# A gated feed-forward's up-projection with both halves of the activation as one 512-column moving operand

## The chip, the cores and the metric

The kernel runs on one core of a Trainium2 chip. The metric is the device time of one execution in microseconds; three executions of the kernel before took 1926.08, 1931.16 and 1932.69 us (median 1931.16). A profile is one further execution, recorded instruction by instruction.

## What is computed

One sequence of 256 tokens, 1024 wide, goes through two blocks of two layers each, all in float32. Six feed-forwards are in it: four gated ones (two in each layer of the first block), which the change touches, and two with a convolution (second block), which it does not touch.

```python
def swiglu(h, w_gate, w_up, w_down):
    return (jax.nn.silu(h @ w_gate) * (h @ w_up)) @ w_down
...
    for i in range(DEPTH):                       # DEPTH = 2
        ...
        h = modulate(rms_norm(x, norm_g[i, 0]), shift[:, 0], scale[:, 0])
        x = x + MACARON_WEIGHT * gate[:, 0, None, :] * swiglu(h, ffn_w_gate[i, 0], ffn_w_up[i, 0], ffn_w_down[i, 0])
        ... # attention
        h = modulate(rms_norm(x, norm_g[i, 2]), shift[:, 2], scale[:, 2])
        x = x + MACARON_WEIGHT * gate[:, 2, None, :] * swiglu(h, ffn_w_gate[i, 1], ffn_w_up[i, 1], ffn_w_down[i, 1])
```

`h` is 256 x 1024, `w_gate` and `w_up` are 1024 x 2816, `w_down` is 2816 x 1024.

## The kernel before

**Numbers in two parts.** TensorE takes its operands as fp32r. Each float32 operand is split into a high part (what fp32r keeps) and a low part (the rest), and a product is made of three matmuls: low activation by high weight, high activation by high weight, high activation by low weight. In the code `h_hi` and `h_lo` are the parts of the activation, `w_hi` and `ring_lo` those of the weight.

**The weight stream.** All weights of the program come in one stream, cut into quarters of 128 x 1024 floats. SyncE loads halves (two quarters) into a ring of four slots. For each quarter ScalarE copies the high part into `w_hi` (L1051, four buffers), and then VectorE subtracts it, in place, to leave the low part in `ring_lo` (L1461). TensorE signals `quarter_done` behind each quarter; ScalarE may split quarter q once quarter q - 4 is done, and SyncE may reload a slot once both of its quarters are done.

**A gated feed-forward** (`ffn` on each engine, called with f = 0 to 3) has 11 steps of up-projection and then 22 quarters of down-projection. A step makes 256 hidden columns of the gate and 256 of the up matrix, from four quarters of weights. `up_turned` holds a 128 x 128 block of weights stationary and streams 256 columns (the tokens) through it: four quarters, two chunks `i` in each, four blocks `b`, three matmuls, so 96 matmuls of 256 columns in a step (L496 to L498). The four blocks accumulate in two banks of PSUM, two blocks side by side: the gate in bank `b`, the up half in bank `b + 1`, with `b` 0 or 2 in turn (`UP_BANKS`). The conv feed-forwards use `up_turned` as well.

**At the end of a step** ScalarE takes the silu of the gate bank into `wa` (L1130), VectorE multiplies it by the up bank into `wb` (L1632, signals `h_ready`), ScalarE copies the high part of the product before this one (`keep_hi`, L1120), and VectorE subtracts to get its low part (`keep`, L1617). Each engine runs its instructions in the order in which they are written: per step ScalarE has four splits, then silu and `keep_hi`; VectorE has four splits with two pieces of other work between them in f = 0 to 2 (`mod_turn`, L1497: columns of the modulation vectors for later layers), then the multiplication and `keep`. Splits run three quarters ahead of TensorE (`LEAD`). TensorE begins step j once `h_ready` of step j - 2 is there.

The **down-projection** (`quarter`, L463 to L465, and `down_last`, L517 to L519) streams 512 columns of weights past a stationary 128 x 128 block of the hidden activation: 12 matmuls of 512 columns in a quarter.

Of the kernel before, what the change touches and what calls it, by code (L numbers as in the profile page):

```python
# [97 lines left out]
POOL_Q = [BASE[_f] + 4 * _j + 5 for _f in ("ffn4", "ffn5") for _j in range(UPS)]  # L98
UP_BANKS = (0, 2)
MIX_BANKS = (0, 2, 4, 0)  # L100
DOWN_BANK = 2
# [71 lines left out]
def build(nc, a, out):  # L173
    ctx = ExitStack()
    with ctx:
# [25 lines left out]
        hT = over("hT", slab_at["hT"], [P, KC, T])  # L201
        h_lo = over("h_lo", slab_at["hT"], [P, KC, T], F32R)
        h_hi = over("h_hi", slab_at["h_hi"], [P, KC, T], F32R)
        arena = over("arena", slab_at["arena"], [P, ARENA])
# [110 lines left out]
        x_ready, x_half = sem("x_ready"), sem("x_half")  # L315
        ms_ready, xn_ready, norm_T, norm_hi, norm_lo = sem("ms_ready"), sem("xn_ready"), sem("norm_T"), sem("norm_hi"), sem("norm_lo")
        silu_ready, h_ready, hid_ready_all = sem("silu_ready"), sem("h_ready"), sem("hid_ready_all")
        fgate_ready, fconv_ready, gelu_ready = sem("fgate_ready"), sem("fconv_ready"), sem("gelu_ready")
# [124 lines left out]
        def _(pe):  # L443
# [39 lines left out]
            def up_turned(q, bank, it, per, fresh):  # L483

                for r in range(4):
# [13 lines left out]
                    mm.then_inc(quarter_done, 1)  # L499

            def down(q, kk, count, parts, bank):

                def lhs(i, tt):
                    return parts(kk, tt)
                quarter(q + kk, None, 0, lhs, lambda i, tt: ps[:, bank + 2 * tt + i, :], lambda i: kk == 0, lambda i: kk == count - 1, kk == count - 1)
# [59 lines left out]
            def ffn(f, conv, m):  # L565
# [3 lines left out]
                def step(j, it):  # L569
                    if v0 + j >= RING or it is not None:  # L570

                        pe.wait_ge(fconv_ready if conv else h_ready, val(it, v0 + j - RING + 1))
                    up_turned(q0 + 4 * j, UP_BANKS[j % 2], it, TURNQ, (norm_lo, 8 * m) if j == 0 else None)

# [8 lines left out]
                for kk in range(DOWNQ):  # L583
                    if kk % 2 == 0:
                        pe.wait_ge(hid_ready_all, UPS * f + kk // 2 + 1)
                    if f < 3 and kk in GATES[f]:
                        gates(*GATES[f][kk])
                    if kk < DOWNQ - TAIL:
                        down(q0 + UPQ, kk, DOWNQ, hid_parts, DOWN_BANK)
# [450 lines left out]
        def _(act):  # L1040
# [81 lines left out]
            def ffn(f):  # L1122
                q0 = BASE[f"ffn{f}"]

                def step(j, it):
                    u, b = UPS * f + j, UP_BANKS[j % 2]
                    split_step(q0 + 4 * j, it, TURNQ)
                    act.wait_ge(quarter_done, val(it, q0 + 4 * j + 4, TURNQ))
                    act.wait_ge(h_ready, val(it, u))
                    nc.scalar.activation(wa[:, 0:512], ps[:, b, :], ACT.Silu).then_inc(silu_ready, 1)  # L1130
                    if j > 0:
                        keep_hi(f, j - 1, it)
                for j in range(PEEL):
# [313 lines left out]
        def _(dve):  # L1447
# [159 lines left out]
            def ffn(f):  # L1607
# [11 lines left out]
                def step(j, it):  # L1619
                    u, b = UPS * f + j, UP_BANKS[j % 2]  # L1620
                    for r in range(4):
                        split(q0 + 4 * j + LEAD + r, q0 + 4 * j + LEAD + r + 1, it, 4 * turn)
                        if mod and r % 2 == 1:
# [4 lines left out]
                            else:  # L1628
                                mod_turn(t, it, MOD_UP * (j - peel) + r // 2)
                    dve.wait_ge(silu_ready, val(it, u + 1, turn))  # L1630
                    half = (j % 2) * 512
                    v.tensor_tensor(wb[:, half:half + 512], ps[:, b + 1, :], wa[:, 0:512], ALU.mult).then_inc(h_ready, 1)  # L1632
                    if j > 0:
                        keep(j - 1, it)

                for j in range(peel):
                    step(j, None)
                with dve.Fori(0, UPS // turn) as it:
                    tick.enter(it, 1 if mod else 0)
                    for r in range(turn):  # L1640
# [698 lines left out]
```

## Time and profile before

| | us |
|---|---|
| median of 3 executions | 1931.16 |
| the profiled execution, its time | 1931.93 |
| its span, first to last instruction | 1930.3 |
| TensorE busy | 1819.3 (94%) |
| VectorE busy | 1420.4 (74%) |
| ScalarE busy | 940.5 (49%) |
| up-projections of the gated feed-forwards | 39 to 168, 398 to 525, 593 to 722, 1115 to 1244 |

The span leaves out 1.6 us around the first and last instruction. The granted TensorE clock has a mean of 0.977 over the span. A matmul's own duration in the trace overlaps with that of its neighbours, so the time that a stream of matmuls takes is read from the distance between their starts.

### The profile page before, as it was taken

To read this page: it belongs to the slowest core of one execution; us is meant where nothing else is said; L and a number is where in the kernel's file an instruction comes from. 1 tells how busy PE (TensorE), PEld (TensorE's weight loads), DVE (VectorE), ACT (ScalarE), POOL (GpSimd) and SP (SyncE) were. 2 spreads that over 40 slices of the span, in tenths; PEclk is the share of its full clock that TensorE was granted. 3 is DMA by queue.
4 is the path that set the end of the run, shared out by engine and by line. 5 is a ranking of instruction groups with operands and counts; after the bars stand their busy time and mean duration, and the time that the engine had idled before them with its cause. 6 is when DMAs were issued, how large, how long until landed. Compare 5 with 4: busy or idle time off the path is not lost.

```text
span 1930.3 us, 31852 instructions
## 1 busy us (share of the span) xinstructions
PE 1819.3 (94%) x11710; PEld 1620.2 (84%) x11710; DVE 1420.4 (74%) x2280; ACT 940.5 (49%) x1360; POOL 128.5 (7%) x168
## 2 busy tenths in 40 slices
PE   2999999889999999999999999999889999979998
PEld 2999777789988997788878799987679987769996
DVE  6778798687778778877665565548869866877894
ACT  3444465454435443555454454445764445664443
POOL 0001010000010000000000000000011100001110
PEclk8999999899999999999999999999999999999999
DMA  9878765457787778454540165545144554324553
GB/s 383 289 277 294 269 230 197 140 186 271 276 306 271 276 267 282 170 175 175 191 155 1 48 233 184 185 175 207 66 177 176 187 185 164 117 88 164 185 180 125
DMA packets 63267, 382.62 MB, mean 198 GB/s; under 512 B 7088, under 2 KB 7088, under 8 KB 26688
## 3 DMA queue, kind: packets, MB, share of 16 engines
q1 hardware_dynamic: 42624, 300.96, 43.3%
q0 software_dynamic: 19984, 77.93, 11.2%
q10 hardware_dynamic: 576, 2.60, 0.3%
q8 instruction: 55, 0.90, 0.2%
q14 instruction: 28, 0.23, 0.0%
HBM read 380.42 MB, written 1.05 MB: 198 GB/s over the span
## 4 chain that ended last, share of the span: by engine, by line
PE 86%; DVE 8%; ACT 4%; issue 2%; DMA 1%; SPq 0%; DVEq 0%; ACTq 0%
PE ps L496 13%; PE ps L497 13%; PE ps L498 13%; PE ps L463 11%; PE ps L465 11%; PE ps L464 11%; DVE ring_lo L1461 1%; PE ps L764 1%; PE ps L517 1%; PE ps L519 1%; PE ps L518 1%; PE ps L790 1%; PE ps L777 1%; PE ps L544 1%; DMA arena<-in_mod 1%
## 5 line engine op out<-in xcount | busy, mean ns | idle before, releaser
L1461 DVE TENSOR_TENSOR ring_lo<-ring,w_hi 128x1024 fp32r<-128x1024 f32 x534 | 647.7, 1222 | 341.4 <-ACT w_hi L1051 336.7
L1051 ACT ACTIVATE w_hi<-ring 128x1024 fp32r<-128x1024 f32 x556 | 584.2, 1057 | 601.2 <-PE ps L498 307.6
L496 PE MATMUL ps<-h_lo,w_hi 128*128 128x256 f32 x2112 | 602.3, 285 | 13.0 <-DVE ring_lo L1461 11.4
L497 PE MATMUL ps<-h_hi,w_hi 128*128 128x256 f32 x2112 | 601.3, 285 | 0.0
L498 PE MATMUL ps<-h_hi,ring_lo 128*128 128x256 f32 x2112 | 600.9, 285 | 0.0
L496 PEld LDWEIGHTS ps<-h_lo,w_hi 128*128 128x128 f32 x2112 | 409.4, 194 | 14.5 <-DVE ring_lo L1461 11.6
L497 PEld LDWEIGHTS ps<-h_hi,w_hi 128*128 128x128 f32 x2112 | 409.5, 194 | 0.0
L498 PEld LDWEIGHTS ps<-h_hi,ring_lo 128*128 128x128 f32 x2112 | 409.2, 194 | 0.0
L463 PE MATMUL ps<-w_hi,h_lo 128*128 128x512 f32 x604 | 246.2, 408 | 13.8 <-DVE h_lo L1873 6.4
L464 PE MATMUL ps<-ring_lo,h_hi 128*128 128x512 f32 x604 | 238.9, 396 | 0.0
L465 PE MATMUL ps<-w_hi,h_hi 128*128 128x512 f32 x604 | 238.7, 395 | 0.0
L463 PE MATMUL ps<-w_hi,hid_lo 128*128 128x512 f32 x456 | 180.0, 395 | 0.0
L465 PE MATMUL ps<-w_hi,hid_hi 128*128 128x512 f32 x456 | 177.5, 389 | 0.0
L464 PE MATMUL ps<-ring_lo,hid_hi 128*128 128x512 f32 x456 | 177.5, 389 | 0.0
L463 PEld LDWEIGHTS ps<-w_hi,h_lo 128*128 128x128 f32 x604 | 115.8, 192 | 42.2 <-issue 8.2
L465 PEld LDWEIGHTS ps<-w_hi,h_hi 128*128 128x128 f32 x604 | 115.6, 191 | 25.4
L464 PEld LDWEIGHTS ps<-ring_lo,h_hi 128*128 128x128 f32 x604 | 115.8, 192 | 22.3
L1497 DVE CUSTOM_DVE_ANT_0 arena<-arena 128x1024 f32<-128x1024 f32 x94 | 114.1, 1219 | 13.8 <-ACT cact L1410 11.1
L405 POOL DMA_DIRECT2D arena<-in_mod x128 | 67.7, 529 | 658.3 <-DVE arena L1497 376.0
L463 PEld LDWEIGHTS ps<-w_hi,hid_lo 128*128 128x128 f32 x456 | 85.6, 188 | 18.9 <-issue 1.2
L464 PEld LDWEIGHTS ps<-ring_lo,hid_hi 128*128 128x128 f32 x456 | 85.6, 188 | 18.8 <-issue 1.4
L465 PEld LDWEIGHTS ps<-w_hi,hid_hi 128*128 128x128 f32 x456 | 85.6, 188 | 17.9
(322 smaller groups left out, 1888.9 us busy)
## 6 DMA issues: line engine op xcount, KB each, us to landing
ring<-in_stream SPq DMA_DIRECT2D x278, 1024.0 KB, 4.8
arena<-in_mod POOLq DMA_DIRECT2D x128, 512.0 KB, 5.6
arena<-in_mod SPq DMA_DIRECT2D x14, 512.0 KB, 15.6
gate<-in_wide POOLq DMA_DIRECT2D x3, 1536.0 KB, 10.0
arena<-in_nsaw POOLq DMA_DIRECT2D x2, 1072.0 KB, 9.2
arena<-in_konst POOLq DMA_DIRECT2D x1, 1295.5 KB, 9.5
arena<-in_mixw POOLq DMA_DIRECT2D x2, 576.0 KB, 10.6
x<-in_x ACTq DMA_DIRECT2D x1, 1024.0 KB, 12.7
```

The source lines that it names most:

```text
L405: pool.dma_start(mring[:, r, :], a["mod"][q, :, r * QUARTER:(r + 1) * QUARTER]).then_inc(mod_in[r], 16)
L463: nc.tensor.matmul(dst, x_lo, hi, start=first(i), stop=False)
L464: nc.tensor.matmul(dst, x_hi, lo, start=False, stop=False)
L465: mm = nc.tensor.matmul(dst, x_hi, hi, start=False, stop=last(i))
L496: nc.tensor.matmul(dst, hi, x_lo, start=(r == 0 and i == 0 and b % 2 == 0), stop=False)
L497: nc.tensor.matmul(dst, hi, x_hi, start=False, stop=False)
L498: mm = nc.tensor.matmul(dst, lo, x_hi, start=False, stop=(r == 3 and i == 1 and b % 2 == 1))
L517: nc.tensor.matmul(dst, x_lo, hi, start=False, stop=False)
L518: nc.tensor.matmul(dst, x_hi, lo, start=False, stop=False)
L1051: nc.scalar.activation(w_hi[:, q % SPLITS, :], ring[:, half % SLOTS, (q % 2) * QUARTER:(q % 2 + 1) * QUARTER], ACT.Copy).then_inc(w_hi_rea ...
L1461: v.tensor_tensor(ring_lo[:, slot, cs], ring[:, slot, cs], w_hi[:, q % SPLITS, :], ALU.subtract).then_inc(w_lo_ready, 1)
L1497: return v.tensor_tensor_reduce(out=junk[n % 2], in0=src, in1=crow, scale=1.0, scalar=0.0, op0=ALU.mult, op1=ALU.add, accum_out=to)
```

## The change

The two parts of the activation become two halves of one tile, `h_both`; in memory they lie where they lay. In steps 1 to 10 of the four gated feed-forwards a new function, `up_wide`, takes the place of `up_turned`. One matmul streams 512 columns, the low and then the high part, through the high weight into one whole PSUM bank; a second one of 256 columns adds high activation by low weight to the upper half of that bank. Each of the four blocks has a bank of its own, and two sets of four banks take turns (`WIDE_BANKS`). What was one sum is now in two halves of a bank. ScalarE copies the lower halves of two banks at a time to `wa`, VectorE adds the upper halves to them, and the silu and the multiplication then read `wa` and not PSUM. Step 0 stays as it was, since it takes the activation as it is made. `gates` in the down-projection uses banks 6 and 7 and so waits for the last step's product.

```diff
+WIDE_BANKS = ((0, 1, 6, 7), (2, 3, 4, 5))
...
-        h_lo = over("h_lo", slab_at["hT"], [P, KC, T], F32R)
-        h_hi = over("h_hi", slab_at["h_hi"], [P, KC, T], F32R)
+        h_both = over("h_both", slab_at["hT"], [P, 2, KC, T], F32R)
+        h_lo, h_hi = h_both[:, 0, :, :], h_both[:, 1, :, :]
...
+            def up_wide(q, banks, it, per):
+
+                for r in range(4):
+                    low_part(q + r, it, per)
+                    slot, half, buf = ((q + r) // 2) % SLOTS, ((q + r) % 2) * QUARTER, (q + r) % SPLITS
+                    for i in range(2):
+                        for b in range(4):
+                            o = i * 512 + b * P
+                            hi, lo = w_hi[:, buf, o:o + P], ring_lo[:, slot, half + o:half + o + P]
+                            nc.tensor.matmul(ps[:, banks[b], :].rearrange("p (w t) -> p w t", w=2), hi, h_both[:, :, 2 * r + i, :],
+                                             start=(r == 0 and i == 0), stop=False)
+                            mm = nc.tensor.matmul(ps[:, banks[b], T:2 * T], lo, h_hi[:, 2 * r + i, :], start=False, stop=(r == 3 and i == 1))
+                    mm.then_inc(quarter_done, 1)
...
+                    if f < 4 and j > 0:
+                        up_wide(q0 + 4 * j, WIDE_BANKS[j % 2], it, TURNQ)
+                        return
                     up_turned(q0 + 4 * j, UP_BANKS[j % 2], it, TURNQ, (norm_lo, 8 * m) if j == 0 else None)
...
                     if f < 3 and kk in GATES[f]:
+                        pe.wait_ge(h_ready, UPS * (f + 1))
                         gates(*GATES[f][kk])
... (ScalarE)
                     act.wait_ge(h_ready, val(it, u))
-                    nc.scalar.activation(wa[:, 0:512], ps[:, b, :], ACT.Silu).then_inc(silu_ready, 1)
-                    if j > 0:
-                        keep_hi(f, j - 1, it)
+                    if j == 0:
+                        nc.scalar.activation(wa[:, 0:512], ps[:, b, :], ACT.Silu).then_inc(silu_ready, 1)
+                        return
+                    for n, b in enumerate(WIDE_BANKS[j % 2][::2]):
+                        low = ps[:, b:b + 2, 0:T]
+                        nc.scalar.activation(wa[:, n * 512:(n + 1) * 512].rearrange("p (b t) -> p b t", b=2), low, ACT.Copy).then_inc(low_kept, 1)
+                    keep_hi(f, j - 1, it)
+                    act.wait_ge(gate_whole, val(it, (UPS - 1) * f + j))
+                    nc.scalar.activation(wa[:, 0:512], wa[:, 0:512], ACT.Silu).then_inc(silu_ready, 1)
... (VectorE)
+                    half = (j % 2) * 512
+                    if j == 0:
+                        dve.wait_ge(silu_ready, u + 1)
+                        v.tensor_tensor(wb[:, half:half + 512], ps[:, b + 1, :], wa[:, 0:512], ALU.mult).then_inc(h_ready, 1)
+                        return
+                    for n, b in enumerate(WIDE_BANKS[j % 2][::2]):
+                        dve.wait_ge(low_kept, val(it, 2 * ((UPS - 1) * f + j - 1) + n + 1, 2 * turn))
+                        low = wa[:, n * 512:(n + 1) * 512].rearrange("p (b t) -> p b t", b=2)
+                        ins = v.tensor_tensor(low, ps[:, b:b + 2, T:2 * T], low, ALU.add)
+                        if n == 0:
+                            ins.then_inc(gate_whole, 1)
+                        else:
+                            tick.mark(ins)
+                    keep(j - 1, it)
                     dve.wait_ge(silu_ready, val(it, u + 1, turn))
-                    half = (j % 2) * 512
-                    v.tensor_tensor(wb[:, half:half + 512], ps[:, b + 1, :], wa[:, 0:512], ALU.mult).then_inc(h_ready, 1)
-                    if j > 0:
-                        keep(j - 1, it)
+                    tick.settle()
+                    v.tensor_tensor(wb[:, half:half + 512], wa[:, 512:1024], wa[:, 0:512], ALU.mult).then_inc(h_ready, 1)
```

How the order of the instructions changes is shown at two places. The first is on TensorE, where step 0 of the first gated feed-forward ends and step 1 begins. Before:

```order
L496 MATMUL ps<-h_lo,w_hi 128x256
L497 MATMUL ps<-h_hi,w_hi 128x256
L498 MATMUL ps<-h_hi,ring_lo 128x256
L496 MATMUL ps<-h_lo,w_hi 128x256 [waits w_lo_ready]
L497 MATMUL ps<-h_hi,w_hi 128x256
```

After (the names of both parts of the activation now read `h_both`):

```order
L498 MATMUL ps<-h_both,w_hi 128x256
L499 MATMUL ps<-h_both,w_hi 128x256
L500 MATMUL ps<-h_both,ring_lo 128x256
L512 MATMUL ps<-h_both,w_hi 128x512 [waits w_lo_ready]
L514 MATMUL ps<-h_both,ring_lo 128x256
```

From step 1 on the three matmuls of a block are two, the first of them twice as wide; the wait for the weight's low part stands where it stood.

The second place is on VectorE, at the end of a step in the loop of the same feed-forward, behind the last piece of modulation work. Before:

```order
L1497 ISA arena<-arena 128x1024 [waits mod_used]
L1497 ISA arena 128x1
L1630 ISA
L1632 TENSOR_TENSOR wb<-ps,wa 128x512 [waits silu_ready]
L1615 REGISTER_ALU
L1617 ISA [waits hid_hi_ready]
L1617 TENSOR_TENSOR hid_lo<-wb,hid_hi 128x512
L1459 REGISTER_ALU
L1461 TENSOR_TENSOR ring_lo<-ring,w_hi 128x1024 [waits w_hi_ready]
```

After:

```order
L1523 ISA arena<-arena 128x1024 [waits mod_used]
L1523 ISA arena 128x1
L1664 TENSOR_TENSOR wa<-ps,wa 128x512 [waits low_kept] x2
L1641 ISA
L1643 ISA [waits hid_hi_ready]
L1643 TENSOR_TENSOR hid_lo<-wb,hid_hi 128x512
L1670 REGISTER_ALU
L164 REGISTER_ALU [waits silu_ready]
L1672 TENSOR_TENSOR wb<-wa 128x512 [waits dve_tick]
L1485 REGISTER_ALU
L1487 TENSOR_TENSOR ring_lo<-ring,w_hi 128x1024 [waits w_hi_ready]
```

Two additions, each with a wait for a copy by ScalarE, stand ahead of everything else at a step's end; the multiplication has moved behind `keep`, and the next quarter's split behind both.

## Rows read from the trace of the kernel before

**Rows 1.** The page: busy time and share of each engine, and the chain's shares.
```profile
span 1930.3 us, 31852 instructions
PE 1819.3 (94%) x11710; PEld 1620.2 (84%) x11710; DVE 1420.4 (74%) x2280; ACT 940.5 (49%) x1360; POOL 128.5 (7%) x168
PE 86%; DVE 8%; ACT 4%; issue 2%; DMA 1%; SPq 0%; DVEq 0%; ACTq 0%
```

**Rows 2.** Busy time by stretch, with count, clock, DMA share, GB/s (steps 1 to 10).
```profile
core 0: us, PE busy (x) PEld busy (x) DVE busy (x) ACT busy (x) POOL busy (x), PEclk, DMA share, GB/s
53.00:168.00 115.00, 115.00 (x961) 115.00 (x960) 84.91 (x104) 51.88 (x59) 10.56 (x20) 1.00 0.77 277
410.00:525.50 115.50, 115.50 (x965) 115.50 (x964) 87.06 (x106) 52.04 (x60) 11.08 (x21) 1.00 0.76 276
1126.00:1244.00 118.00, 118.00 (x984) 117.96 (x983) 62.89 (x60) 54.12 (x62) 0.00 (x0) 1.00 0.51 182
```

**Rows 3.** Waits in 53 to 168 us: total us, times, longest.
```profile
POOL arena L405 <- DVE arena L1497: 99.0, 19, 5.2
ACT w_hi L1051 <- PE ps L498: 44.4, 30, 1.8
DVE ring_lo L1461 <- ACT w_hi L1051: 27.9, 30, 1.7
ACT wa L1130 <- PE ps L498: 17.6, 10, 1.9
```

**Rows 4.** Timeline of ScalarE (start us, duration us): four silus, a step apart.
```profile
87.69 0.60 ACT L1130 ACTIVATE wa<-ps 128x512 f32<-128x512 f32 x1 [1.91 <-PE ps L498]
...
122.24 0.60 ACT L1130 ACTIVATE wa<-ps 128x512 f32<-128x512 f32 x1 [1.90 <-PE ps L498]
```

**Rows 5.** Timeline of TensorE: up-projection's end, down-projection's start and last matmul of L465.
```profile
1243.36 0.28 PE L497 MATMUL ps<-h_hi,w_hi 128*128 128x256 f32 x1
1243.48 0.28 PE L498 MATMUL ps<-h_hi,ring_lo 128*128 128x256 f32 x1
1243.60 0.40 PE L463 MATMUL ps<-w_hi,hid_lo 128*128 128x512 f32 x1
...
1295.08 0.39 PE L465 MATMUL ps<-w_hi,hid_hi 128*128 128x512 f32 x1
```

**Rows 6.** Timeline of TensorE: from 512 columns to 256, and to a smaller stationary block.
```profile
1401.96 0.40 PE L465 MATMUL ps<-w_hi,h_hi 128*128 128x512 f32 x1
1402.19 1.02 PE L1010 MATMUL ps<-arena 128*128 128x256 f32 x4
...
309.68 0.39 PE L465 MATMUL ps<-w_hi,h_hi 128*128 128x512 f32 x1
310.00 0.81 PE L670 MATMUL ps<-arena 64*128 64x256 f32 x6
```

**Rows 7.** Groups by line: count, busy us, mean ns of one.
```profile
L1461 DVE TENSOR_TENSOR ring_lo<-ring,w_hi 128x1024 fp32r<-128x1024 f32 x534 | 647.7, 1222 | 341.4 <-ACT w_hi L1051 336.7
L1632 DVE TENSOR_TENSOR wb<-ps,wa 128x512 f32<-128x512 f32 x44 | 30.4, 691 | 16.0 <-ACT wa L1130 13.9
L1130 ACT ACTIVATE wa<-ps 128x512 f32<-128x512 f32 x44 | 26.4, 600 | 78.0 <-PE ps L498 78.0
L1120 ACT ACTIVATE hid_hi<-wb 128x512 f32 x40 | 24.9, 622 | 0.0
L1690 DVE SCALAR_TENSOR_TENSOR wb<-ps,cols,wb 128x255 f32<-128x255 f32 x88 | 38.0, 473 | 0.0
```

**Rows 8.** Timeline of VectorE around the end of a step of the first gated feed-forward.
```profile
98.47 1.22 DVE L1497 CUSTOM_DVE_ANT_0 arena<-arena 128x1024 f32<-128x1024 f32 x1
99.62 0.08 DVE L1497 DVE_READ_ACCUMULATOR2_ANT arena<- 128x1 f32 x1
99.85 0.17 DVE L1549 COPY arena<-arena 128x4 f32 x1 [0.16 <-DVE arena L1497]
99.96 0.69 DVE L1632 TENSOR_TENSOR wb<-ps,wa 128x512 f32<-128x512 f32 x1
100.57 0.68 DVE L1617 TENSOR_TENSOR hid_lo<-wb,hid_hi 128x512 f32 x1
101.29 1.23 DVE L1461 TENSOR_TENSOR ring_lo<-ring,w_hi 128x1024 fp32r<-128x1024 f32 x1
```

**Rows 9.** Timeline of ScalarE at the same step's end.
```profile
99.20 0.60 ACT L1130 ACTIVATE wa<-ps 128x512 f32<-128x512 f32 x1 [1.90 <-PE ps L498]
99.69 0.62 ACT L1120 ACTIVATE hid_hi<-wb 128x512 f32 x1
100.21 1.05 ACT L1051 ACTIVATE w_hi<-ring 128x1024 fp32r<-128x1024 f32 x1
```

More of the change, by code:

```diff
@@ L316, in build @@
         ms_ready, xn_ready, norm_T, norm_hi, norm_lo = sem("ms_ready"), sem("xn_ready"), sem("norm_T"), sem("norm_hi"), sem("norm_lo")
+        low_kept, gate_whole = sem("low_kept"), sem("gate_whole")
         silu_ready, h_ready, hid_ready_all = sem("silu_ready"), sem("h_ready"), sem("hid_ready_all")
@@ L1638, in ffn @@
                 with dve.Fori(0, UPS // turn) as it:
-                    tick.enter(it, 1 if mod else 0)
+                    tick.enter(it, (1 if mod else 0) + turn)
                     for r in range(turn):
```

## The prediction

> **What bounds the kernel now.** I read the page's head first: TensorE is busy for 94% of the span and carries 86% of the chain that ended last [rows 1]. Such a share is a mean, so the stretches that the change touches come next. In steps 1 to 10 of the gated feed-forwards TensorE is busy without a break (115.00 of 115.00 us), at the full clock, in the feed-forwards with modulation work as in the one without, while VectorE is busy 84.91 us, ScalarE 51.88 and the DMA engines 0.77 of the time [rows 2]. The list of waits of that stretch holds no wait of TensorE at all: the others wait, VectorE for ScalarE's splits, and ScalarE for TensorE to free its buffers [rows 3]. So only what shortens TensorE's own work counts here, until another engine's work for a step is longer than TensorE's.
>
> **What a matmul costs.** Three steps lie between the first and last silu shown, 122.24 - 87.69 = 34.55 us, or 11.52 a step; with 96 matmuls in a step one takes 120.0 ns [rows 4]. The 512-column matmuls of a down-projection: from 1243.60 to 1295.08 lie 227 distances (19 quarters of 12), 51.48 us, so 226.8 ns each [rows 5]. At 2.4 GHz, the level that a granted clock of 1.00 stands for, 256 columns need 106.7 ns and 512 need 213.3. Both kinds leave the same rest, 13.3 and 13.4 ns. I read it as a fixed part of each matmul that does not grow with the columns.
>
> **Part 1, three matmuls become two.** A block's group took 3 x 120.0 = 360.0 ns; it now takes 226.8 + 120.0 = 346.8, and 13.2 ns go. There are 4 feed-forwards x 10 steps x 8 chunks x 4 blocks = 1280 groups, so 1280 x 13.2 ns = 16.9 us. The streamed columns are the same (768 a group); only one fixed part is saved. A step becomes 32 x 346.8 = 11.10 us, 0.42 less.
>
> The trace of before has no stream in which both widths alternate, so the pair is bounded by rows. That a switch of width can be free is seen both ways: 256 columns followed by 512 start 0.12 us apart, 512 followed by 256 on a full block 0.23 [rows 5, 6]. The dearest switch in the rows is 0.32 us, from a 512-column matmul to one on a 64-row block [rows 6]; that would add 0.09 to each group. At the cheap end the 256-column matmul loses its rest too (106.7 ns, a group of 333.5), and 1280 x 26.5 = 33.9 us go. I take the free switch, since the new pair keeps one block shape and one type.
>
> The Trainium skill, "TensorE: Matmul & The Clock Gate", section "Back-to-back issue gap", gives N / 2.4 + 2.5 ns for a warm matmul, so 109.2 ns for 256 columns and 215.8 for 512. The rows show 120.0 and 226.8, so the trace does not agree: the rest is 13.3 here, not 2.5. By the page a group would save 2.5 ns and the change an estimated 3.2 us.
>
> **Part 2, the copies on ScalarE.** Two copies of 512 elements from PSUM are added to each step, 2 x 0.60 by the silu that reads as much from there [rows 7]. ScalarE has 5.2 us of work in a step (51.88 / 10, rows 2); with 1.2 more it is 6.4 of 11.10. Nothing on the path by volume.
>
> **Part 3, the additions on VectorE.** Two of 512 elements with one operand in PSUM, 0.69 each by the multiplication of that shape [rows 7]. VectorE's 8.5 us a step (84.91 / 10) become 9.9 of 11.10, 89%. The dearer bound is 0.95 each, from 473 ns for 255 elements out of PSUM [rows 7]; that makes 10.4. The multiplication reads SBUF now and keeps 0.69. So volume hides it in either case, with 0.7 to 1.2 us to spare in a step of the three feed-forwards with modulation work. The fourth has 62.89 us of VectorE work in 118.00, and far more room [rows 2].
>
> **Part 4, the longer way at a step's end.** This is an added wait, so I follow who stands behind it. Before, with TensorE's step ending at about 99.15, silu runs 99.20 to 99.80, the product 99.96, `keep` 100.57, and the split of the quarter after is done at 102.52, 3.4 us behind the step's end [rows 8, 9]. After: ScalarE's two copies end at 0.65 and 1.15 us; VectorE is free from its modulation work at about 0.9 (99.85 + 0.17, a tenth later since the step is shorter), adds until 1.6 and 2.2, `keep` ends at 2.9; ScalarE's silu, which must wait for the first addition, runs 1.7 to 2.3; the product ends at 3.6, and the split, which queues behind it, at 4.8. That is 1.4 us later. What waits for it: this split is of the last quarter of the step that TensorE has just begun, three quarters of 2.77 us further on, so it is needed at 8.3. It has 3.5 us to spare. ScalarE's split of that quarter moves from about 2.1 to 3.4 us behind the step's end and is done before VectorE asks. From 4.8 VectorE works 1.2 (split), 1.3 (modulation) and 1.2 (split), and it is at 8.5 when ScalarE's fourth split (allowed at 8.3, done at 9.5) makes it wait again. So it has caught up within the step, and nothing adds up from step to step.
>
> TensorE itself waits for the product of two steps before; that comes 3.6 us behind its step's end, against 11.10. The wait added ahead of `gates` wants the last product, 3.6 us into the down-projection; the earliest place is three quarters in, 3 x 12 x 0.227 = 8.2 us. Both at nothing. If this cover were gone, each microsecond of it would be paid once in a step. DMA: the same bytes in 96.4% of the time, 277 to 287 GB/s at a share near 0.80 [rows 2]. Nothing.
>
> **The sum.** 1931.93 (the profiled execution) - 16.9 = 1915.0 us. The median of before is 0.8 below that execution, so I expect 1914.3 as a median.
>
> **The rivals.**
>
> A. *The fixed part does not go.* The 512 columns come from two pieces 2048 elements apart, and they are written as two runs. If the rest of 13.3 ns is paid per run of 256 columns, the group stays at 360 ns: 1931. For it: the rows' 512-column matmuls all stream one unbroken piece. Against it: nothing in the rows says that it is paid per run. 0.08. The rule of the Trainium skill cited above would end near it, with an estimate of 3.2 us saved, 1928; the rows' rest of 13.3 ns speaks against that one.
>
> B. *Each switch of width costs.* The 0.32 of rows 6, so 0.09 more for each of 1280 groups, less 16.9: 115 - 17 = 98 us slower, 2029. It decides from 13 ns a group on. Against it stand the two free switches [rows 5, 6]. 0.04.
>
> C. *VectorE becomes the bound.* It decides for a loss where its work and forced waits in a step exceed 11.52 us, so where the additions and the waits between them cost 3.0 us rather than the 1.4 counted. For it: it is already the second engine, and the new order makes VectorE and ScalarE wait for each other twice. At 12.0 us a step, 30 steps would lose 0.5 each against now, 15 us, and the fourth feed-forward would win 4: about 1942. Against it: 0.7 us to spare even at the dearer bound. 0.06. A milder form, in which VectorE sets a step of 11.3, gives 1921; I count 0.06.
>
> D. *More goes than forecast*, the cheap end of part 1: 1897. It needs the 256-column matmul to be held at 120 ns now by what surrounds it, not by itself. 0.06.
>
> **How the numbers follow.** The forecast has 0.70. The range of 8 in 10 holds the forecast's own spread (three executions of before span 6.6 us) and the mild form of C, and reaches halfway to D: 1906 to 1923. What a measurement of this kernel can tell from no change is about 0.3%, 5.8 us. Faster by more: 0.70 + 0.06 (mild C) + 0.06 (D) + 0.02 (the part of A and C that falls beyond it) = 0.84. Within: 0.08. Slower: 0.08, from B and C.
>
> **What would show it.** Starts of a 512-column and the following 256-column matmul 227 and 120 ns apart in steps 1 to 10, silus 11.1 us apart (part 1); A would show 240 and 120, B a distance of 0.3. No wait of TensorE for `ring_lo` in those stretches (C). VectorE at about 0.89 there, additions of 0.69 and copies of 0.60, its fourth split still waiting for ScalarE. The down-projections and all else the same to a microsecond. The prediction is wrong if the pair takes other than 0.347 us, or if TensorE waits at a step's beginning.

## The result

The changed kernel takes 1918.45 us (median of four executions, 1917.88 to 1920.4) against 1931.93 for the kernel before in the same comparison: a ratio of 0.9937 with a 95% interval of 0.9913 to 0.996. So 13.5 us went. The forecast was 1914.3, inside a range of 1906 to 1923 that holds the measured median. The profiled execution took 1918.12 us, 13.8 less than the profiled one of before.

The page of the changed kernel: head, shares of the chain, and the two new groups of TensorE (count, busy us, mean ns of one).

```profile
span 1916.5 us, 29564 instructions
PE 1805.1 (94%) x10430; PEld 1546.6 (81%) x10430; DVE 1461.6 (76%) x2360; ACT 977.2 (51%) x1440; POOL 128.6 (7%) x168
PE 86%; DVE 7%; ACT 4%; issue 2%; DMA 1%; SPq 0%; DVEq 0%; ACTq 0%
L512 PE MATMUL ps<-h_both,w_hi 128*128 128x512 f32 x1280 | 452.5, 399 | 0.0
L514 PE MATMUL ps<-h_both,ring_lo 128*128 128x256 f32 x1280 | 359.5, 281 | 0.0
```

Beside [rows 1]: 1280 matmuls are gone (11710 to 10430), VectorE and ScalarE have 80 instructions more each and 41 and 37 us more work, and TensorE still carries 86% of the chain.

The changed kernel's windows (columns as in rows 2) over most of steps 1 to 10 of the first gated feed-forward, and its waits in the same stretch (us in total, times, longest):

```profile
53.00:160.00 107.00, 107.00 (x607) 92.74 (x606) 89.97 (x117) 58.01 (x75) 10.03 (x19) 1.00 0.80 281
```

```profile
ACT w_hi L1071 <- PE ps L514: 31.2, 19, 1.8
ACT wa L1155 <- PE ps L514: 16.6, 9, 1.9
DVE ring_lo L1487 <- ACT w_hi L1071: 15.8, 11, 1.6
```

TensorE is busy without a break and at the full clock, as in [rows 2], and no wait of TensorE is in the list, as in [rows 3]. VectorE went from 74% of the stretch to 84%. What TensorE does in a group is therefore again all that counts. Its timeline (start us, duration us): the first and last pair of steps 1 to 10, and three pairs between them.

```profile
52.80 0.40 PE L512 MATMUL ps<-h_both,w_hi 128*128 128x512 f32 x1
53.03 0.28 PE L514 MATMUL ps<-h_both,ring_lo 128*128 128x256 f32 x1
...
100.15 0.40 PE L512 MATMUL ps<-h_both,w_hi 128*128 128x512 f32 x1
100.39 0.28 PE L514 MATMUL ps<-h_both,ring_lo 128*128 128x256 f32 x1
100.50 0.40 PE L512 MATMUL ps<-h_both,w_hi 128*128 128x512 f32 x1
100.73 0.28 PE L514 MATMUL ps<-h_both,ring_lo 128*128 128x256 f32 x1
100.85 0.40 PE L512 MATMUL ps<-h_both,w_hi 128*128 128x512 f32 x1
101.09 0.28 PE L514 MATMUL ps<-h_both,ring_lo 128*128 128x256 f32 x1
101.21 0.40 PE L512 MATMUL ps<-h_both,w_hi 128*128 128x512 f32 x1
...
165.75 0.28 PE L514 MATMUL ps<-h_both,ring_lo 128*128 128x256 f32 x1
165.87 0.40 PE L465 MATMUL ps<-w_hi,hid_lo 128*128 128x512 f32 x1
```

From 52.80 to 165.87 lie 113.07 us and 320 pairs: **353.3 ns a pair**, where 346.8 was forecast. The three pairs between 100.15 and 101.21 show it too: 1.06 us. Ten steps before took 115.20 us (960 x 120.0). So a feed-forward won 2.13 us and the four won 8.5, half of the 16.9 forecast. Where the other 5.3 us of the profiled executions went is followed below, with the clock, as far as the traces show it.

### The profile page after: what moved, and what is told of

It is laid out like the page before. It is cut to its first block, busy times and chain, and to the rows that moved or that the text cites. A ratio compares the mean times of both kernels' runs of the same rounds, so it can differ in the third digit from the quotient of the medians.

```text
span 1916.5 us, 29564 instructions
## 1 busy us (share of the span) xinstructions
PE 1805.1 (94%) x10430; PEld 1546.6 (81%) x10430; DVE 1461.6 (76%) x2360; ACT 977.2 (51%) x1440; POOL 128.6 (7%) x168
## 3 DMA queue, kind: packets, MB, share of 16 engines
q0 software_dynamic: 19984, 77.93, 11.4%
## 4 chain that ended last, share of the span: by engine, by line
PE 86%; DVE 7%; ACT 4%; issue 2%; DMA 1%; SPq 0%; DVEq 0%; ACTq 0%
PE ps L512 16%; PE ps L465 11%; PE ps L467 11%; PE ps L466 11%; PE ps L514 8%; PE ps L498 5%; PE ps L499 5%; PE ps L500 5%; PE ps L533 1%; DVE ring_lo L1487 1%; PE ps L535 1%; PE ps L534 1%; PE ps L784 1%; PE ps L810 1%; PE ps L560 1%
## 5 line engine op out<-in xcount | busy, mean ns | idle before, releaser
L512 PE MATMUL ps<-h_both,w_hi 128*128 128x512 f32 x1280 | 452.5, 399 | 0.0
L514 PE MATMUL ps<-h_both,ring_lo 128*128 128x256 f32 x1280 | 359.5, 281 | 0.0
L512 PEld LDWEIGHTS ps<-h_both,w_hi 128*128 128x128 f32 x1280 | 240.5, 188 | 60.1
L465 PE MATMUL ps<-w_hi,h_both 128*128 128x512 f32 x604 | 246.7, 408 | 13.5 <-DVE h_both L1911 6.4
L498 PE MATMUL ps<-h_both,w_hi 128*128 128x256 f32 x832 | 237.7, 286 | 13.1 <-DVE ring_lo L1487 11.0
L514 PEld LDWEIGHTS ps<-h_both,ring_lo 128*128 128x128 f32 x1280 | 241.8, 189 | 0.0
L466 PE MATMUL ps<-ring_lo,h_both 128*128 128x512 f32 x604 | 238.8, 395 | 0.0
L467 PE MATMUL ps<-w_hi,h_both 128*128 128x512 f32 x604 | 238.7, 395 | 0.0
L499 PE MATMUL ps<-h_both,w_hi 128*128 128x256 f32 x832 | 236.9, 285 | 0.0
L500 PE MATMUL ps<-h_both,ring_lo 128*128 128x256 f32 x832 | 236.6, 284 | 0.0
L465 PE MATMUL ps<-w_hi,hid_lo 128*128 128x512 f32 x456 | 180.0, 395 | 0.0
L498 PEld LDWEIGHTS ps<-h_both,w_hi 128*128 128x128 f32 x832 | 161.3, 194 | 14.6 <-DVE ring_lo L1487 11.4
L499 PEld LDWEIGHTS ps<-h_both,w_hi 128*128 128x128 f32 x832 | 161.4, 194 | 0.0
L500 PEld LDWEIGHTS ps<-h_both,ring_lo 128*128 128x128 f32 x832 | 161.3, 194 | 0.0
L465 PEld LDWEIGHTS ps<-w_hi,h_both 128*128 128x128 f32 x604 | 115.8, 192 | 41.6 <-issue 9.2
L467 PEld LDWEIGHTS ps<-w_hi,h_both 128*128 128x128 f32 x604 | 115.6, 191 | 25.3
L466 PEld LDWEIGHTS ps<-ring_lo,h_both 128*128 128x128 f32 x604 | 116.3, 192 | 22.5
```

Source lines behind the costliest of these rows:

```text
L465: nc.tensor.matmul(dst, x_lo, hi, start=first(i), stop=False)
L466: nc.tensor.matmul(dst, x_hi, lo, start=False, stop=False)
L467: mm = nc.tensor.matmul(dst, x_hi, hi, start=False, stop=last(i))
L498: nc.tensor.matmul(dst, hi, x_lo, start=(r == 0 and i == 0 and b % 2 == 0), stop=False)
L499: nc.tensor.matmul(dst, hi, x_hi, start=False, stop=False)
L500: mm = nc.tensor.matmul(dst, lo, x_hi, start=False, stop=(r == 3 and i == 1 and b % 2 == 1))
```

## The experiments

After the result two reasons were open for the missing 6.7 ns a pair. **The runs**: the 512 moving columns are two pieces and go to PSUM as two halves of 256 (a milder rival A). **The switch**: a matmul whose neighbour has another width costs more (rival B's mechanism, at a fraction of its price). Beside them stood the eviction work, on ScalarE and VectorE, that the prediction hid at no cost. Diffs are against the changed kernel. All of them are timed beside executions of the kernel before on the same chip; a time given without a ratio is that of a single execution.

**The changed kernel once more.**

> The changed kernel once more, beside the experiments. In its first profile a pair of a 512-column and a 256-column matmul took 353.3 ns, not 346.8, so 1280 x 6.7 = 8.5 us are saved there; the whole span fell by 13.8 us, and the other 5.2 went with time at the half clock (92.7 us before, 65.7 after). Theory 'clock by chance': pair again 353.3 ns, time 1918 to 1924, and the part of the difference beyond 8.5 us follows the mean granted clock of the run. Theory 'clock by the change': the half-clock time is again near 65 us and that of the kernel before again near 90.

1918.84 us, ratio 0.9936 (0.9919 to 0.9952), again 353.3 ns a pair. The gain and the size of the pair repeat. The two theories on the clock fail. The profile has about 79 us at the lower clock, where 65 was expected if the change itself set it (92 before, 65 in the first profile). And the part beyond 8.5 us does not follow the mean granted clock: among executions with a mean of 0.981 in this comparison, those of before took 1931.0 to 1931.3 us and those of this kernel 1916.5 to 1919.0, a difference of about 12.6.

**The 512 columns in one unbroken piece, read and written in one run.** What is shown is the heart of the edit; the instructions that write and read `h_both` elsewhere follow the new layout.

```diff
-        h_both = over("h_both", slab_at["hT"], [P, 2, KC, T], F32R)
-        h_lo, h_hi = h_both[:, 0, :, :], h_both[:, 1, :, :]
+        h_both = over("h_both", slab_at["hT"], [P, KC, 2 * T], F32R)
+        h_lo, h_hi = h_both[:, :, 0:T], h_both[:, :, T:2 * T]
...
-                            nc.tensor.matmul(ps[:, banks[b], :].rearrange("p (w t) -> p w t", w=2), hi, h_both[:, :, 2 * r + i, :],
+                            nc.tensor.matmul(ps[:, banks[b], :], hi, h_both[:, 2 * r + i, :],
```

> The two halves of the activation lie side by side for each chunk, so that the 512 columns are one unbroken run of memory and the output is written as one run; all else as in the changed kernel. Theory 'runs' (the missing 6.7 ns of a pair are paid because operand and output come as two runs of 256): pair 346.7 ns, 8.5 us faster than the changed kernel, about 1910. Theory 'switch' (paid because neighbouring matmuls have different widths): pair stays at 353.3, time as the changed kernel, 1918.

Timeline of TensorE in this kernel, from the first matmul of 512 columns to the last:

```profile
53.16 0.40 PE L512 MATMUL ps<-h_both,w_hi 128*128 128x512 f32 x1
...
165.87 0.40 PE L512 MATMUL ps<-h_both,w_hi 128*128 128x512 f32 x1
```

319 pairs in 112.71 us, 353.3 ns each, and 1918.49 us in all (ratio 0.9937, 0.992 to 0.9953). Nothing moved, so the runs cost nothing. Rival A is out as well: with the fixed part paid twice a pair would take 360 ns.

**Four matmuls of 512 columns, then four of 256, in each chunk.** The same matmuls with a quarter of the switches.

```diff
                         for b in range(4):
                             o = i * 512 + b * P
-                            hi, lo = w_hi[:, buf, o:o + P], ring_lo[:, slot, half + o:half + o + P]
-                            nc.tensor.matmul(ps[:, banks[b], :].rearrange("p (w t) -> p w t", w=2), hi, h_both[:, :, 2 * r + i, :],
+                            nc.tensor.matmul(ps[:, banks[b], :].rearrange("p (w t) -> p w t", w=2), w_hi[:, buf, o:o + P], h_both[:, :, 2 * r + i, :],
                                              start=(r == 0 and i == 0), stop=False)
+                        for b in range(4):
+                            o = i * 512 + b * P
+                            lo = ring_lo[:, slot, half + o:half + o + P]
                             mm = nc.tensor.matmul(ps[:, banks[b], T:2 * T], lo, h_hi[:, 2 * r + i, :], start=False, stop=(r == 3 and i == 1))
```

> Within a chunk the four 512-column matmuls come first and then the four 256-column ones, so that the width changes twice in eight matmuls and not eight times; operands as in the changed kernel. Theory 'switch': 4 x 346.7 + 6.7 = 1393.3 ns for eight, or 348.3 a pair, 6.4 us faster than the changed kernel, about 1912. Theory 'runs': 353.3 a pair as before, about 1918.

Timeline of TensorE, the first and last row of four wide matmuls:

```profile
52.48 0.40 PE L511 MATMUL ps<-h_both,w_hi 128*128 128x512 f32 x1
...
163.34 1.09 PE L511 MATMUL ps<-h_both,w_hi 128*128 128x512 f32 x4
```

79 chunks in 110.86 us, 1403.3 ns for eight matmuls, 350.8 a pair; 1914.72 us (ratio 0.9922, 0.9904 to 0.994). Fewer switches do cost less, but not a quarter of 6.7: against 4 x (226.7 + 120.0) = 1386.7 ns a chunk has 16.7 too many for its two switches, where a pair has 6.7 for its two.

**Both edits together**, the two diffs above.

> Both edits together: the 512 columns as one unbroken run of memory, and four 512-column matmuls ahead of four 256-column ones. With fours alone eight matmuls took 1403.3 ns, 16.7 more than four at 226.7 and four at 120.0; inside the four wide ones the starts stood 233, 236, 228, 233 ns apart. Theory 'switch' (the 16.7 ns belong to the two changes of width): 1403.3 again, about 1914.5. Theory 'runs in a row of wide ones' (the 233 instead of 227 is paid for the broken operand, which alternation hid): 1386.7 for eight, 2.7 us faster than fours alone, about 1912.

1403.3 ns a chunk again, 1915.87 us (ratio 0.9917, 0.99 to 0.9933). The layout of the columns makes no difference in this order either.

**Eight and eight**, one row of each width in a quarter; first one execution, then six more of the same kernel.

```diff
                     for i in range(2):
                         for b in range(4):
...
+                    for i in range(2):
+                        for b in range(4):
+                            o = i * 512 + b * P
+                            lo = ring_lo[:, slot, half + o:half + o + P]
                             mm = nc.tensor.matmul(ps[:, banks[b], T:2 * T], lo, h_hi[:, 2 * r + i, :], start=False, stop=(r == 3 and i == 1))
```

> For each quarter eight 512-column matmuls and then eight 256-column ones, operands as in the changed kernel. Theory 'switch': 16 matmuls take 2773.3 + 16.7 = 2790.0 ns, or 348.8 a pair, 16.6 ns less than two blocks of fours for each of 160 quarters, 2.7 us, so about 1912. Theory 'each wide matmul is dearer by itself': 2806.6 ns as two blocks of fours, about 1914.5.

Timeline of TensorE, first and last row of eight wide matmuls:

```profile
52.75 0.40 PE L511 MATMUL ps<-h_both,w_hi 128*128 128x512 f32 x1
...
161.69 2.00 PE L511 MATMUL ps<-h_both,w_hi 128*128 128x512 f32 x8
```

The one execution took 1921.46 us. 39 quarters in 108.94 us, 2793.3 ns for sixteen matmuls: 20.0 over 8 x 346.7, and neither of the two numbers expected, though 3.3 from the nearer. The distances inside show why. Behind a switch the wide matmuls follow each other by 233, 236, 229, 232, 231, 227, 226, 227 ns, and the first narrow one by 113 and then 119 and 120. The first five wide matmuls are 28 ns dearer in all than five at 226.7, and the first two narrow ones give 8 back. In shorter rows less of it is paid: the next narrow matmul comes before the fifth wide one.

> The kernel with eight wide and eight narrow matmuls in turn once more, timed (it was looked at once, at a mean clock of 0.977, with 1921.46 us). Its trace has 2793.3 ns for sixteen matmuls, 20.0 more than eight at 226.7 and eight at 120.0, against 26.7 in eight matmuls of the changed kernel. Theory 'the time follows TensorE's stream': 160 blocks of sixteen x (8 x 353.3 - 2793.3 = 33.3 ns) = 5.3 us less than the changed kernel, about 1913.5. Rival 'the later use of the low weights or the moved quarter ends cost it back': 1918 or more.

1917.7 us over six executions (1912.36 to 1922.17; ratio 0.9928, 0.9908 to 0.9948). The shorter stream of TensorE is there (349.2 ns a pair), yet the time is hardly below that of the changed kernel. The rival of the expectation, a cost of the later low weights or the moved quarter ends, is not what the trace shows: in the profiled execution steps 1 to 10 won 13.9 us and everything else together lost 0.1. What is missing is the further gain that the changed kernel had outside these steps; see the clock, below.

**Every matmul 512 columns wide.** The second one streams both parts too, so this kernel adds the product of both low parts to the sum.

```diff
-                            mm = nc.tensor.matmul(ps[:, banks[b], T:2 * T], lo, h_hi[:, 2 * r + i, :], start=False, stop=(r == 3 and i == 1))
+                            mm = nc.tensor.matmul(ps[:, banks[b], :].rearrange("p (w t) -> p w t", w=2), lo, h_both[:, :, 2 * r + i, :], start=False, stop=(r == 3 and i == 1))
```

> The order of the changed kernel, but the second matmul of a group streams 512 columns as well (low and high activation by the low weight; the product of both low parts is added to what is computed). No width ever changes. Theory 'switch': 2 x 226.7 = 453.3 ns a group, 100.0 more than 353.3, so 1280 x 0.100 = 128 us slower, about 2047. Theory 'each wide matmul that goes to another bank or comes in two runs is dearer': 2 x 233.3 = 466.7 ns or something between, up to 2064.

Timeline of TensorE, first and last:

```profile
52.80 0.40 PE L512 MATMUL ps<-h_both,w_hi 128*128 128x512 f32 x1
...
197.89 0.39 PE L465 MATMUL ps<-w_hi,hid_lo 128*128 128x512 f32 x1
```

640 matmuls in 145.09 us, 226.7 ns each, and 2047.78 us in all. Same layout, same banks, same eviction work, no switch inside the stretch: nothing is left of the surcharge but the one lot at its start (233, 236, 228, 232 and 231 ns, then 227). This and the rows of four and eight show that it comes with the change of width.

**The wide matmul taken apart again**, with all the copies and additions kept.

```diff
-                            nc.tensor.matmul(ps[:, banks[b], :].rearrange("p (w t) -> p w t", w=2), hi, h_both[:, :, 2 * r + i, :],
-                                             start=(r == 0 and i == 0), stop=False)
+                            nc.tensor.matmul(ps[:, banks[b], 0:T], hi, h_lo[:, 2 * r + i, :], start=(r == 0 and i == 0), stop=False)
+                            nc.tensor.matmul(ps[:, banks[b], T:2 * T], hi, h_hi[:, 2 * r + i, :], start=False, stop=False)
```

> The changed kernel with its banks, copies and additions, but the 512-column matmul is taken apart again into two of 256 columns (low activation into the lower half of the bank, high activation into the upper). It has all that the change adds on ScalarE and VectorE and nothing of what it takes from TensorE. Theory 'the new work is hidden': 360 ns a group, 8.5 us slower than the changed kernel, so about 1927 to 1932, within 0.3% of the kernel before. Rival 'the longer way at a step's end costs': slower than the kernel before by over 6 us, with waits of TensorE for ring_lo. If a bank of its own for each block costs on TensorE, the group is over 360 ns.

Timeline of TensorE, first matmul of step 1 and first of the down-projection, and the windows of the stretch:

```profile
52.70 0.28 PE L512 MATMUL ps<-h_both,w_hi 128*128 128x256 f32 x1
...
167.90 0.40 PE L465 MATMUL ps<-w_hi,hid_lo 128*128 128x512 f32 x1
```

```profile
53.00:160.00 107.00, 107.00 (x894) 107.00 (x894) 88.11 (x116) 57.03 (x75) 10.04 (x19) 1.00 0.79 276
```

960 matmuls in 115.20 us, 120.0 each as in [rows 4]; 1931.57 us over ten executions, ratio 1.0005 (0.9996 to 1.0015). The whole new eviction, on its own, costs nothing that can be measured, at most 0.15%. It had steps of 11.52 us here, not 11.31; whether it also fits into the shorter ones is asked next.

**How much cover is left.** Two, then four further additions of 512 elements on VectorE in each step, with one operand in PSUM, their result unused, each waited for. The edit of the second; the first leaves out the factor 2:

```diff
+                    for b in WIDE_BANKS[j % 2][::2] * 2:
+                        spare, ones2 = [w.rearrange("p (b t) -> p b t", b=2) for w in (wc[:, 512:1024], konst[:, 0:512])]
+                        tick.mark(v.tensor_tensor(spare, ps[:, b:b + 2, T:2 * T], ones2, ALU.add))
+                        tick.settle()
                     keep(j - 1, it)
```

> The changed kernel with two more additions at each step's end. With four more the first three gated feed-forwards became slower, 31 us in all. VectorE has about 9.5 us of work in a step of 11.31; this makes it about 11.0. Theory 'only volume over TensorE's step counts': the time stays at 1918 to 1920 and TensorE waits for no ring_lo in steps 1 to 10. Rival 'the way at a step's end is already near its limit': over 6 us slower.

> The changed kernel with four more additions of the same shape on VectorE at each step's end, ahead of keep, each waited for; their result is used by nobody. VectorE worked about 9.5 us in a step of 11.31 us in the first three feed-forwards; this makes it about 12.4, more than TensorE's. Theory 'VectorE's volume is what counts': VectorE sets the pace there, 30 steps x about 1.1 = 33 us slower than the changed kernel, about 1951, with waits of TensorE for ring_lo; in the fourth, without modulation work, about 9.2 us stay hidden and nothing changes. Rival 'the waits between the engines set the pace before volume does': over 40 us slower, and the fourth slower too.

The windows of the same stretch, with two more and then with four more, and of the latter one line of its waits over the whole span:

```profile
53.00:160.00 107.00, 107.00 (x608) 92.83 (x607) 100.14 (x134) 57.58 (x76) 10.02 (x19) 1.00 0.82 281
```

```profile
53.00:160.00 107.00, 100.67 (x565) 86.08 (x565) 100.61 (x137) 54.26 (x69) 8.97 (x17) 1.00 0.73 265
PE ps L512 <- DVE ring_lo L1487: 22.0, 24, 1.2
```

With two more VectorE is at 94% and the time stays (1917.19 us). With four more it cannot keep up: TensorE is busy 100.67 of 107.00 us and waits for `ring_lo`, 24 times, and the time is 1949.66 us. The busy share reads 94% in both. What tells them apart is TensorE's wait, not the share. The ten steps of the first three feed-forwards grow from 113.07 to about 121.7 us each, 26 us in all; the fourth, with no modulation work, stays at 113.07. That is what the volume theory said (1951 us forecast, the fourth unchanged). So rival C is a true limit in the three feed-forwards with modulation work, between two and four additions above the changed kernel.

**Rows of sixteen.** In every second quarter the narrow matmuls come first, so that rows of the same width meet.

```diff
+                    if r % 2 == 0:
+                        wide()
+                        mm = narrow()
+                    else:
+                        narrow()
+                        mm = wide()
                     mm.then_inc(quarter_done, 1)
```

> Every other quarter streams its narrow matmuls first, so that sixteen narrow ones and sixteen wide ones stand together and the width changes four times in a step and not eight. Theory 'a fixed 20 ns for each pair of changes once the rows of one width are long': 32 matmuls take 5546.7 + 20.0 = 5566.7 ns, 40 steps x 40 ns = 1.6 us less than eights, about 1912. Theory 'the excess grows with the length of the rows' (6.7, 16.7 and 20.0 ns for rows of one, four and eight): over 25 ns for sixteens, and no gain over eights.

Timeline of TensorE: first row, a row of each width, and the end of step 10.

```profile
53.01 2.00 PE L512 MATMUL ps<-h_both,w_hi 128*128 128x512 f32 x8
...
156.96 3.82 PE L512 MATMUL ps<-h_both,w_hi 128*128 128x512 f32 x16
160.62 2.08 PE L521 MATMUL ps<-h_both,ring_lo 128*128 128x256 f32 x16
...
164.37 0.39 PE L465 MATMUL ps<-w_hi,hid_lo 128*128 128x512 f32 x1
```

111.36 us for ten steps: 11.14 a step, where 32 x 346.7 ns and two pairs of switches at 20.0 make 11.13. This version has the lowest median: 1911.78 us (1911.09 to 1911.91), ratio 0.9901 (0.9882 to 0.992), 19.6 us below the kernel before. Its interval overlaps that of fours (0.9904 to 0.994).

**The clock at step 0.** The first step of a feed-forward is the same code before and after. Its windows in the third and fourth gated feed-forward (14 us, from 0.4 to 0.7 us ahead of its first matmul) and the 6 us ahead of each (the normalization, in which TensorE pauses and does 16 small matmuls). Before:

```profile
586.50:592.50 6.00, 3.90 (x20) 2.85 (x19) 5.61 (x12) 5.00 (x13) 1.66 (x3) 0.82 0.90 303
592.50:606.50 14.00, 13.44 (x97) 13.29 (x97) 13.69 (x23) 8.89 (x12) 0.53 (x1) 0.84 0.77 287
1108.40:1114.40 6.00, 3.50 (x19) 2.41 (x17) 5.53 (x12) 5.05 (x14) 1.62 (x3) 0.84 0.92 302
1114.40:1128.40 14.00, 13.57 (x97) 13.60 (x97) 12.22 (x20) 8.44 (x11) 0.00 (x0) 0.82 0.78 313
```

The changed kernel:

```profile
580.60:586.60 6.00, 3.09 (x20) 2.08 (x19) 5.61 (x12) 5.13 (x14) 1.66 (x3) 1.00 0.84 296
586.60:600.60 14.00, 13.26 (x106) 13.06 (x107) 13.69 (x23) 10.12 (x14) 0.53 (x1) 1.00 0.78 293
1099.25:1105.25 6.00, 3.89 (x18) 3.17 (x16) 5.44 (x12) 4.51 (x12) 1.63 (x3) 0.72 0.90 340
1105.25:1119.25 14.00, 13.65 (x108) 13.35 (x108) 13.03 (x22) 10.24 (x14) 0.00 (x0) 1.00 0.79 303
```

The kernel with eight and eight, third and fourth:

```profile
585.60:599.60 14.00, 13.43 (x97) 13.29 (x97) 13.69 (x23) 8.88 (x12) 0.53 (x1) 0.84 0.80 291
1104.00:1118.00 14.00, 13.52 (x96) 13.55 (x97) 12.27 (x20) 8.47 (x11) 0.00 (x0) 0.82 0.75 300
```

The third number from the right is the granted clock. Before, and with eight and eight, step 0 starts at half the clock (1.2 GHz); in the changed kernel both have the full 2.4 GHz throughout. The time from the first matmul of step 0 to the first of step 1 shrinks from 13.29 to 11.59 us in the third feed-forward, from 13.57 to 11.59 in the fourth, and by 0.3 in the other two together: 4.0 us in all. What decides it was not settled. In 13 profiles, the third step 0 begins at the lower clock in six and the fourth in six; the repeat of the changed kernel has the lower one in the third, and so the same code can go either way. The second one can too: it takes 11.7 to 11.9 us in ten of the profiles and 13.4 in three, those of the changed kernel once more, of one piece with fours, and of sixteens. In all five profiles where TensorE's stream is that of before or of eight and eight, or all wide, the third and fourth both begin low.

The stream's own saving and the measured one, side by side (medians; the stream's is 1280 x (360.0 - ns a pair), for sixteens 40 x (11.52 - 11.13) us):

| kernel | ns a pair | stream, us | measured, us | rest |
|---|---|---|---|---|
| changed | 353.3 | 8.5 | 13.5 | 5.0 |
| changed, once more | 353.3 | 8.5 | 12.4 | 3.9 |
| one piece | 353.3 | 8.5 | 12.8 | 4.3 |
| fours | 350.8 | 11.8 | 16.5 | 4.7 |
| one piece, fours | 350.8 | 11.8 | 14.8 | 3.0 |
| eight and eight | 349.2 | 13.8 | 13.7 | -0.1 |
| sixteens | 347.9 | 15.5 | 19.6 | 4.1 |
| taken apart | 360.0 | 0 | -0.3 | -0.3 |

The rest is 3 to 5 us, and nothing in the two kernels whose profile shows the lower clock in both places. The profiled executions say where it lay. In this table all is read from the starts of TensorE's matmuls and is the difference to the profile of before, in us:

| kernel | won in all | steps 1 to 10 | the four steps 0 | elsewhere |
|---|---|---|---|---|
| changed | 13.8 | 8.5 | 4.0 | 1.3 |
| changed, once more | 11.4 | 8.5 | 0.8 | 2.1 |
| one piece | 13.0 | 8.5 | 3.5 | 1.0 |
| fours | 18.0 | 11.7 | 4.1 | 2.1 |
| one piece, fours | 13.9 | 11.7 | 0.6 | 1.6 |
| eight and eight | 13.8 | 13.9 | 0.2 | -0.2 |
| sixteens | 20.3 | 15.4 | 2.0 | 2.8 |
| taken apart | 0.5 | 0 | 0.5 | 0 |

So step 0 alone is not the whole of it. In two of the kernels with a rest (the changed one once more, one piece with fours) it gave under 1 us, and the largest piece elsewhere lies between the first down-projection's start and the second step 0: 230.5 us long before (mean granted clock 0.95), 228.9 in the changed kernel (0.96) and 227.5 in the one with sixteens (0.97), with the same instructions. In both places the shorter time has the higher granted clock. That the clock makes the rest is therefore likely and not shown: these are single executions, no kernel was made that sets the clock alone, and why the kernels with another stream tend to get more of it is open.

## Why the prediction was right, and where it was not

**What bounds the kernel** held: TensorE's own stream in steps 1 to 10, before and after.

**The matmuls alone** held within 0.1 ns: 120.0 ns for 256 columns and 226.7 for 512 in streams of one width (taken apart, all wide). The rule of the Trainium skill, "TensorE: Matmul & The Clock Gate", section "Back-to-back issue gap", which the page gives for a matmul's gap in isolation, has 109.2 and 215.8 ns. The trace agrees with neither; by the rule an estimated 3.2 us would have gone, and the stream alone gave 8.5.

**Part 1 is the step that failed**, in its choice of the free switch. Its term, 1280 x 13.2 = 16.9 us, measured 1280 x 6.7 = 8.5. By the prediction's own sign ("wrong if the pair takes other than 0.347 us") this part was wrong: the pair takes 353.3 ns. The mechanism was rival B's, at 6.7 ns a pair where B was priced at 90 from a switch that also changed the block's shape; from 13 ns on the change would have been a loss. The two rows read as free [rows 5, 6] could not show it: each is one distance, printed to 10 ns, and the surcharge lies in the wide matmuls behind a switch (235, 232, 241 ns in the pairs), while the narrow one even comes early (114 to 120). The trace of before did hold the surcharge, a few rows on:

```profile
1244.76 0.39 PE L465 MATMUL ps<-w_hi,hid_hi 128*128 128x512 f32 x1
```

From the first wide matmul at 1243.60 [rows 5] to this sixth one lie 1.16 us, where five distances of 226.7 ns make 1.13. To the nanosecond they are 233, 236, 228, 233 and 231, as in the rows of eight. So the sum for two widths has to be read over several matmuls behind the switch, not over one distance.

**Part 2 and part 3** held. The groups of the new instructions in the changed kernel (count, busy us, mean ns of one, idle time ahead):

```profile
L1664 DVE TENSOR_TENSOR wa<-ps,wa 128x512 f32<-128x512 f32 x80 | 51.5, 686 | 13.5 <-ACT wa L1155 12.2
L1155 ACT ACTIVATE wa<-ps 128x512 f32<-128x512 f32 x80 | 43.5, 597 | 73.9 <-PE ps L514 73.9
L1672 DVE TENSOR_TENSOR wb<-wa 128x512 f32<-128x512 f32 x40 | 27.4, 686 | 0.0
```

Additions 0.69 us and copies 0.60, as costed. VectorE's work in a step is 89.97 / 107.00 x 11.31 = 9.5 us (84%) where 9.9 (89%) was counted. A halved operand over two banks costs no more than one bank.

**Part 4** held. VectorE and ScalarE at a step's end in the changed kernel:

```profile
99.10 1.28 DVE L1664 TENSOR_TENSOR wa<-ps,wa 128x512 f32<-128x512 f32 x2
100.30 0.68 DVE L1643 TENSOR_TENSOR hid_lo<-wb,hid_hi 128x512 f32 x1
100.90 0.68 DVE L1672 TENSOR_TENSOR wb<-wa 128x512 f32<-128x512 f32 x1
101.50 1.22 DVE L1487 TENSOR_TENSOR ring_lo<-ring,w_hi 128x1024 fp32r<-128x1024 f32 x1
```

```profile
98.31 1.09 ACT L1155 ACTIVATE wa<-ps 128x512 f32<-128x512 f32 x2 [1.85 <-PE ps L514]
99.28 0.64 ACT L1140 ACTIVATE hid_hi<-wb 128x512 f32 x1
99.82 0.63 ACT L1158 ACTIVATE wa<-wa 128x512 f32<-128x512 f32 x1
```

The product ends 3.3 us behind the step's end (about 98.27) and the split 4.5, where 3.6 and 4.8 were forecast, against [rows 8, 9]. No wait of TensorE came of it, and the kernel taken apart puts its price at nothing.

**The sum** missed for two reasons with opposite signs. Of the profiled executions' 13.8 us, the pairs gave 8.5 (8.4 less than forecast), step 0, with its higher clock, gave 4.0 that was not forecast, and 1.3 fell elsewhere: 0.7 in step 0 of the two conv feed-forwards, and 0.6 as the net of 1.6 won ahead of the second feed-forward and about 1.0 lost in other places. With the pairs alone the time would be near 1923, at the very edge of the range. That the median lies well inside it is luck: it owes this to a gain that the prediction did not have, in places that the change does not touch.

## What to carry to other kernels

Merging two matmuls over the same stationary block saves one fixed part, 13.3 ns here, no matter that the columns lie in two pieces; but a merge that leaves its neighbours at another width gives half of it back (6.7 ns here), so put matmuls of one width in long rows (sixteen here) where banks and buffers allow it. In this kernel the second engine's added work was free as long as no wait for it showed on the first: test that with the work added alone, and with more of it than needed. Compare a saving with the stream's own distances before believing the total, since a clock that changes level elsewhere can add or hide microseconds.

## What the hardware showed unexpectedly

- Two changes of width between neighbouring matmuls cost 6.7 ns in rows of one, 16.7 in rows of four, 20.0 in rows of eight and about 20 in rows of sixteen: a surcharge on the first five wide matmuls behind a switch (28 ns in rows of eight), given back in small part (8 ns) by the first two narrow ones. Where in TensorE it arises was not tried.
- A moving operand in two pieces of 256 columns streams at 226.7 ns, as an unbroken one.
- The same code of step 0 began at 1.2 GHz in some profiles and at 2.4 in others, for 1.6 to 2.0 us each. In the 6 us ahead of it TensorE ran the same 20 matmuls before and after in the third feed-forward, with the clock at 0.82 in the one (3.90 us of work) and 1.00 in the other (3.09). A low clock there does not settle it either: ahead of the fourth the changed kernel had 0.72, and its step 0 ran at 1.00.
